# Finding the dropped keys instead of the kept ones: sparse-attention selection on 384 keys in 16 rounds, with those rows last

## The reference, cut to what matters

```
score = jnp.einsum('bqh,bqhs->bqs', wi, jax.nn.relu(dots))
score = jnp.where(mask, score, NEG_BIG)       # block-causal, chunks of 64
_, sel = lax.top_k(score, n_sel)              # prompt 256, sample 136
...                                           # softmax over the selected keys, times values
```

## Time and profile before

| | |
|---|---|
| runs | 3884.03, 3888.84, 3899.14 us; median 3888.84 |
| profiled execution | 3897.18 us, span 3895.3 us |
| mean granted TensorE clock | 0.971 of full speed |

### The profile page before, as it was taken

One profiled execution on the slowest core, in us unless ns is written; L12 is line 12 of the kernel. 1 busy time (PEld: TensorE's weight loads), 2 busy tenths in 40 slices (PEclk: granted clock), 3 DMA queues, 4 the chain that ended last, 5 costly groups with the idle time before them and its releaser, 6 DMA issues. The chain is left out here.

```text
span 3895.3 us, 54785 instructions
## 1 busy us (share of the span) xinstructions
PE 3691.7 (95%) x21676; PEld 2940.2 (75%) x21676; DVE 2065.7 (53%) x4711; ACT 1263.7 (32%) x2918; POOL 761.1 (20%) x812
## 2 busy tenths in 40 slices
PE   7997799999999999999999999999999999999998
PEld 5775577678777777778867777787777787788887
DVE  1674564376635554428846555067644654553442
ACT  1124333245243432222244333145344433312221
POOL 2200211111010133202000013323001011453334
PEclk9998898999999999999999999999999999999999
DMA  4332222322121223233231222335112122342223
GB/s 146 97 109 65 77 87 78 103 95 92 56 84 36 78 89 96 80 113 124 72 101 48 82 68 88 107 114 162 55 48 87 30 84 65 96 141 87 67 84 94
DMA packets 151608, 339.55 MB, mean 87 GB/s; under 512 B 30312, under 2 KB 68648, under 8 KB 138040
## 3 DMA queue, kind: packets, MB, share of 16 engines
q1 hardware_dynamic: 151352, 336.04, 27.7%
HBM read 299.31 MB, written 36.68 MB: 86 GB/s over the span
## 5 line engine op out<-in xcount | busy, mean ns | idle before, releaser
L1042 PE MATMUL PS<-xn,wring 128*128 128x272 f32 (+1 forms) x7168 | 1693.7, 396 | 24.9 <-DVE xn L1598 15.1
L1042 PEld LDWEIGHTS PS<-xn,wring 128*128 128x128 f32 x7168 | 1381.1, 195 | 288.6 <-issue 35.3
L2010 POOL TENSOR_TENSOR xT<-xT,res 128x272 f32<-128x272 f32 (+1 forms) x320 | 255.6, 800 | 2251.3 <-ACT res L1325 2211.4
L1042 PE MATMUL PS<-dense,wring 128*128 128x256 f32 (+1 forms) x2816 | 654.6, 390 | 10.4 <-ACT res L1325 5.1
L1042 PEld LDWEIGHTS PS<-dense,wring 128*128 128x128 f32 x2816 | 532.1, 192 | 106.7 <-issue 10.3
L1325 ACT ACTIVATE res<-PS 128x272 f32<-128x272 f32 (+1 forms) x320 | 123.6, 388 | 539.5 <-PE PS L1042 514.0
L1063 PE MATMUL PS<-wring,xn 128*128 128x256 f32 (+1 forms) x1152 | 266.3, 392 | 2.3 <-ACT dense L1339 2.3
L1063 PEld LDWEIGHTS PS<-wring,xn 128*128 128x128 f32 (+1 forms) x1152 | 214.4, 188 | 49.5 <-issue 5.9
L1042 PE MATMUL PS<-catT,wring 128*128 128x272 f32 (+1 forms) x1024 | 235.5, 391 | 4.7 <-issue 2.7
L1333 ACT ACTIVATE dense<-PS 128x256 f32<-128x256 f32 (+1 forms) x176 | 68.3, 389 | 521.7 <-PE PS L1042 480.9
L1042 PEld LDWEIGHTS PS<-catT,wring 128*128 128x128 f32 x1024 | 195.2, 192 | 44.8 <-issue 11.3
(11 more groups left out here) (243 smaller groups left out, 4492.7 us busy)
## 6 DMA issues: line engine op xcount, KB each, us to landing
wring<-in_wu SPq DMA_DIRECT2D x88, 1024.0 KB, 4.9
wring<-in_wf SPq DMA_DIRECT2D x88, 512.0 KB, 3.7
wring<-in_wo SPq DMA_DIRECT2D x64, 512.0 KB, 3.6
wring<-in_wd SPq DMA_DIRECT2D x96, 320.0 KB, 2.9
wring<-in_wd SPq DMA_DIRECT2D x64, 384.0 KB, 3.1
wring<-in_wn SPq DMA_DIRECT2D x16, 1024.0 KB, 5.5
kv<-out_projT SPq DMA_DIRECT2D x48, 256.0 KB, 4.2
out_projT<-dense SPq DMA_DIRECT2D x40, 272.0 KB
```

What stands on the lines that cost most here:

```text
L1042: mm = nc.tensor.matmul(PS[:, dbank(t.g0), 0:cw], wtile(t.q, i), rhs, start=(kk == a), stop=(kk == b - 1))
L2010: nc.gpsimd.tensor_tensor(x, x, res[:, i % NRES, 0:cw], ALU.add).then_inc(s_res, 1)
```

## The change

For the unit with 384 keys (`few_go`), 384 - 256 = 128 keys are to be dropped. Its scores are negated into the unit's place in `bias`, 16 rounds run there instead of 32, and the last maximum of the last round, negated, is the bound. Eight instructions then settle the ties as lines 1752 to 1759 do for second halves, and write the bias. The units are sorted so that this one comes third: 512 keys, 544 keys (sample), 384 keys. `ROUNDS[0]` becomes 32, 17, 16; X has 41 steps and not 49, and the planner, which reads `ROUNDS`, places all steps of passes 0 and 2 anew.

```diff
+def few_go(u):
+    return u.prompt and u.nk < 2 * TOP_P
-PICKS = [[u for u in UNITS[h] if u.nk > 2 * P] for h in range(2)]
-ROUNDS = [[(TOP_P if u.prompt else TOP_S) // 8 for u in PICKS[h]] for h in range(2)]
+PICKS = [sorted((u for u in UNITS[h] if u.nk > 2 * P), key=few_go if h == 0 else lambda u: 0) for h in range(2)]
+ROUNDS = [[(u.nk - TOP_P if few_go(u) else TOP_P if u.prompt else TOP_S) // 8 for u in PICKS[h]] for h in range(2)]
...
-                    wk = work[:u.w, 0:u.nk]
+                    x = work[:u.w, 0:u.nk]
+                    wk = kept(u) if few_go(u) else x
+                    if z == 0 and few_go(u):
+                        step(nc.vector.tensor_scalar(wk, x, -1.0, None, ALU.mult))
                     for r in range(BURST * z, min(BURST * z + BURST, ROUNDS[h][y])):
                         step(nc.vector.max(top[:u.w, :], wk))
                         step(nc.vector.match_replace(wk, top[:u.w, :], wk, SENTINEL))
-                    if BURST * z + BURST >= ROUNDS[h][y]:
+                    if BURST * z + BURST >= ROUNDS[h][y] and few_go(u):
+                        bound = cand[:, 0:1]
+                        same, rank = rl[:, 0, 0:u.nk], rl[:, 1, 0:u.nk]
+                        step(nc.vector.tensor_scalar(bound, top[:, 7:8], -1.0, None, ALU.mult))
+                        step(nc.vector.tensor_scalar(rank, x, bound, None, ALU.is_gt, ALU.add, accum_out=count[:, 0:1]))
+                        step(nc.vector.tensor_scalar(same, x, bound, None, ALU.is_equal))
+                        step(nc.vector.tensor_scalar(least[:, 0:1], count[:, 0:1], -1.0, float(TOP_P), ALU.mult, ALU.add))
+                        step(nc.vector.tensor_tensor_scan(rank, same, same, 0.0, ALU.add, ALU.max))
+                        step(nc.vector.scalar_tensor_tensor(same, rank, least[:, 0:1], same, ALU.is_gt, ALU.mult))
+                        step(nc.vector.scalar_tensor_tensor(rank, x, bound, same, ALU.is_lt, ALU.add))
+                        nc.vector.tensor_scalar(wk, rank, 8 * NEG, None, ALU.mult).then_inc(x_bias, 1)
+                    elif BURST * z + BURST >= ROUNDS[h][y]:
                         nc.vector.tensor_scalar(bias[:u.w, u.bias:u.bias + u.nk], wk, SENTINEL, 8 * NEG, ALU.not_equal, ALU.mult)\
                             .then_inc(x_bias, 1)
```

## The result

The changed kernel takes 3903.07 us (median of 20 runs, 3894.63 to 3908.31), the kernel before beside it 3890.36 us (20 runs). The ratio is 1.0034, 95% interval 1.0025 to 1.0042: slower by a third of a per cent, some 13 us, and 5 us above the range that was forecast. The profiled execution took 3904.39 us.

What follows compares the result with a forecast made beforehand. Selection was taken as TensorE-bound, pass 0's attention and recurrence as bound by TensorE and waits in turn. Gains of 6.5 us (pass 0) and 2.5 (pass 2) made 3888.84 - 9 = 3880, own range 3873 to 3884, whole range 3862 to 3898.

Steps and rivals of the forecast that it cites:

- The work on VectorE: Selection of the 384-key unit: 16.4 us saved in pass 0, about 16 in pass 2, with closing instructions taken at 4.2.
- The planner: Dense turns leave selection for attention, recurrence and norms: 13.0 us (about 3.6 turns) in pass 0, 17.9 (five) in pass 2.
- The two arrive together: Start of attention in pass 0: TensorE arrives and VectorE ends the selection at about 239 us, so attention waits no longer than before.
- The unit's new place in the order costs nothing by itself: Start of selection: the 512-key unit, now first, adds some tenths of a us, which TensorE's next turns cover.
- signs that I had named for being wrong: TensorE waiting at attention's first matmul, the norm's two waits growing, or idle time staying while later stretches lengthen by 13 us.
- The loads for B: Attention's loads in pass 0: issued about 14.8 us ahead of it instead of 18, which still covers.
- Pass 0: Dense turns moved into attention, recurrence and norms fill waits, 5 us, and win back clock: 6 to 8 us, taken as 6.5.
- Five turns at under 1 us each, with no clock to win, 2.5 us: Pass 2: five dense turns leave the full selection stretch and fill thinly spread idle time of 25.5 us, gaining 2.5 us.
- Slower: Rival, chance 0.12: the second half's norm inside pass 0's attention waits longer for ScalarE; 3895 to 3903 us.
- the two that I had named: TensorE's waits for ScalarE's squares in pass 0's norm block, 1.89 and 2.65 us; the slower case had both reach 6.7.
- Nothing comes of it: Rival, chance 0.20: TensorE is the busy engine and later stretches grow by all that selection sheds; 3889 us, 3884 to 3894.

## Why the prediction was wrong

**The work on VectorE: right.** 1.25 us for a round and 4.15 us for the closing chain, against 4.2. That it is worth next to nothing in X was right too: 2 us with the old places, and not clear of noise.

**The planner: right in direction.** In pass 0 B begins at turn 57 and not 60. In pass 2 it begins seven turns earlier, where five were forecast, as a turn of that FFN costs 2.9 of the planner's units on average, and not the 3.6 that I divided by.

**"The two arrive together": wrong, and without effect.** TensorE came 1.4 us earlier than forecast and VectorE 3 us later. Some 2 of these are longer waits for ReLUs (1.8, 0.8 and 3.95 us for the three units, against 1.4, 2.6 and 0.8 before); where the third comes from is not shown. "The unit's new place in the order costs nothing by itself" had looked at the unit that now comes first and not at the one that comes last. TensorE waited 5.4 us, one of the signs that I had named for being wrong. Cutting that wait to 2 us gained nothing. The loads for B are issued 14.1 us ahead of it (the first at 223.48 us), and nothing waited for them there; 14.8 were forecast.

**Pass 0: right in sign and near in size, and the size by luck.** 6.5 us were forecast and 7.7 to 10.9 measured. The sum was waits filled in B, C and M, and clock won back behind them. (It was loose, too: 7.2 to 3.6 us with the clock in proportion make 12 to 6, not 8 to 6.) Neither term is there. Idle time didn't fall from 67 to 60 us; it is 481.3 - 415.1 = 66.2 us, and the granted clock is 0.91, where the four kernels with pass 0 at exactly the old turns, the kernel before among them, have 0.89 to 0.93. B, C and M take 480 to 481 us in eight kernels with the new turns, and 465 to 482 in these four (472 at the median), so by the medians most of what came in was paid for. The gain is in X, which is 14 to 15 us shorter: some 11 are the three turns that left, and 4 are the wait for the first ReLUs, 3.7 to 4.5 us with the new turns and 7.4 to 8.2 with the old. The forecast had looked at that place only for what the larger unit adds to it. The Trainium skill ("TensorE: Matmul & The Clock Gate", "What's actually happening") has activity release the clock. Pass 0 doesn't show it: 48 matmuls more, and a clock inside the range of the old turns. The late stretch of pass 2 agrees with it: 13.9 us of idle time and not 20.3, and 0.96 and not 0.92.

**Pass 2: the step that failed.** "Five turns at under 1 us each, with no clock to win, 2.5 us" turned out as a loss of 18 to 26 us. I had treated the turns that move as filler and asked only what they fill. They are places in the order as well. All 59 steps of B moved forward by three to eight turns and 26 of the 30 of C by one to four, past FFN turns, which have work of their own on VectorE and ScalarE, and some landed ahead of it: six steps of C make 11.8 us, shown by repair (3903.07 to 3891.27, one turn later). Putting the fault into the kernel before gives the size (+10.3) and two of the four waits. And a stretch at 0.99 has no clock to win but clock to lose: it fell to 0.95, and of the 14.0 us in the late stretch 7.7 are matmuls at the lower clock. Some 4 us of C's 16 and most of the 10 us of X and B have no place that I could show, and their cause stays open; the entry of B accounts for 4 of them by one run, whose interval overlaps that of the change, and for none by another.

**The rivals.** "Slower" gave 3895 to 3903 and the time is 3903, but its place was the norm block of pass 0, and pass 0 gained. The norm's longest wait did grow (from 2.80 us to 6.71 for the normalized rows, at 375.69 us), the two that I had named hardly did (1.89 and 2.65 us to 2.55 and 2.45), and that pass still came out ahead. "Nothing comes of it" is what the version at the old turns shows, 3888.

**The better version.** The new selection with the old need for pass 2 takes 3880.69 us, 0.17% (0.04 to 0.30) under the kernel before. That was the time I had forecast for the change, by chance: it is what the change gives when pass 2 stays where it was, and the forecast had 2.5 us of pass 2 in it and other terms for pass 0.

## What to carry to other kernels

When an edit makes a hand- or planner-placed order move, don't price the moved work alone: list, for each moved step, what else its engines have to issue at the turn where it lands, who waits for that, and what the moved step itself waits for, since everything behind it in its queue waits too. Six steps one turn too early cost 11.8 us, more than 38.7 us less work on VectorE ever gave. Price a full stretch by what it has to lose in idle time and clock. Change the work and the places separately on the chip before you keep either, since here the work was worth 2 us at the median, and the places lost 18 to 26 us in one pass and gained 8 to 11 in the other. And compare a stretch with more than one execution of the old order: here the one that was read first was the longest of four.

## What the runs showed of the hardware

Matmuls at the lower clock can follow waits that are shorter than the dense turns around them, and need not. After 3.49 us the next 22 matmuls took 6.70 us (0.30 us each), while after 1.33 us, in the version with six steps later, ten of the same matmuls took 2.40 us (0.24 each). A wait of 5.37 us was followed by a dense turn of 6.39 us, where the next one took 3.83. But one and the same wait went both ways: after 2.30 us ahead of turn 532, 32 matmuls took 8.72 us in the changed kernel and 7.17, full speed, in the version with X and B at the old turns. So the length of a wait alone doesn't tell. On balance the late stretch of pass 2, with 6.3 us more idle time, is 14.0 us longer: there the waits cost about twice their length. A reciprocal of 128x544 on VectorE takes 3.55 us, more than four times a pass with two tensor sources of that size (0.72 to 0.79 us).
